# A hybrid decoder step on one core: attention's first tiles, mask and ones placed outside the staging memory

## The reference

```python
def stick_breaking_weights(z, mask):
    log_beta = jax.nn.log_sigmoid(z)
    log_1m = jnp.where(mask, jax.nn.log_sigmoid(-z), 0.0)
    ax = z.ndim - 1
    tail = lax.cumsum(log_1m, axis=ax, reverse=True) - log_1m
    return jnp.where(mask, jnp.exp(log_beta + tail), 0.0)

def block(args):                       # 128 queries, all keys
    q_blk, start = args
    z = einsum('bqhd,bkhd->bhqk', q_blk, k) * scale + bias
    mask = kpos[None, :] < (start + arange(128))[:, None]
    a = stick_breaking_weights(z, mask)
    return einsum('bhqk,bkhd->bqhd', a, v)
```

## Time and profile before

| | |
|---|---|
| median of 3 runs | 2984.35 us (2983.45 to 2986.84) |
| the profiled execution | 2984.83 us, its span 2983.1 us |
| busy, share of the span | PE 93%, PEld 89%, DVE 43%, POOL 35%, ACT 22% |
| granted TensorE clock, mean | 0.95 |
| chain that ended last | PE 82%, DVE 9%, issue 5%, ACT 3% |
| Q projection to first attention matmul | about 1571 to 1654 us |
| attention, 144 chunks | about 1654 to 1937 us |
| decode step | about 1937 to 2091 us |

### The profile page before, as it was taken

The page is one execution under the profiler, slowest core; times in us unless marked ns, Lnnn a source line. Parts: engine busy times, 40 slices in busy tenths (PEclk is TensorE's granted clock), DMA queues, the critical chain, the costliest instruction groups (busy, mean ns, idle before and its releaser), DMA issues.

```text
span 2983.1 us, 42739 instructions
## 1 busy us (share of the span) xinstructions
PE 2786.8 (93%) x16800; PEld 2646.7 (89%) x16800; DVE 1278.5 (43%) x2082; ACT 647.0 (22%) x1248; POOL 1036.2 (35%) x742
## 2 busy tenths in 40 slices
PE   4999859999999999989999899989999999999997
PEld 3777529899999999989989799978989999999997
DVE  6589975522222222264133688700352222222226
ACT  4111134300000000023122688700130000000002
POOL 2267952132322232222222566601223322233220
PEclk9999879999999999999999899955999999999999
DMA  3000001021111111114415434243101111111111
GB/s 125 26 19 28 8 36 43 22 64 43 44 49 43 43 45 55 43 39 143 139 51 153 124 104 114 61 145 106 43 24 62 43 50 43 43 43 52 48 43 59
DMA packets 80413, 184.08 MB, mean 62 GB/s; under 512 B 25811, under 2 KB 40531, under 8 KB 79988
## 3 DMA queue, kind: packets, MB, share of 16 engines
q1 hardware_dynamic: 56980, 145.00, 15.7%
q10 hardware_dynamic: 23264, 36.61, 4.1%
HBM read 150.59 MB, written 30.99 MB: 61 GB/s over the span
## 4 chain that ended last, share of the span: by engine, by line
PE 82%; DVE 9%; issue 5%; ACT 3%; POOL 0%; ACTq 0%; DVEq 0%; DMA 0%; SPq 0%; POOLq 0%
PE bank L1179 50%; PE bank L1283 15%; PE bank L1384 4%; DVE cv L937 3%; PE bank L1368 2%; PE bank L1440 2%; PE bank L1412 2%; PE bank L1224 1%; PE bank L1355 1%; PE bank L1356 1%; DVE xg L882 1%; DVE xl L886 1%; DVE ssq L872 1%; PE bank L1246 0%; DVE x L1153 0%
## 5 line engine op out<-in xcount | busy, mean ns | idle before, releaser
L1179 PE MATMUL bank<-xh,wh 128*128 128x352 f32 x3456 | 1130.6, 327 | 32.5 <-DVE xl L886 22.9
L1179 PE MATMUL bank<-xh,wl 128*128 128x352 f32 x3456 | 1116.2, 323 | 0.0
L1179 PE MATMUL bank<-xl,wh 128*128 128x352 f32 x3456 | 1116.1, 323 | 0.0
L489 POOL CAST wh<-w_raw 128x1024 fp32r<-128x1024 f32 x188 | 282.7, 1503 | 1654.4 <-PE bank L1179 1394.4
L1179 PEld LDWEIGHTS bank<-xh,wh 128*128 128x128 f32 x3456 | 654.3, 189 | 45.4 <-DVE xl L886 18.3
L1179 PEld LDWEIGHTS bank<-xl,wh 128*128 128x128 f32 x3456 | 656.7, 190 | 1.8 <-issue 1.7
L1179 PEld LDWEIGHTS bank<-xh,wl 128*128 128x128 f32 x3456 | 655.4, 190 | 0.0
L491 POOL TENSOR_TENSOR wl<-w_raw,wh 128x1024 fp32r<-128x1024 f32 x188 | 456.3, 2427 | 15.0
L1004 DVE TENSOR_TENSOR bank<-bank,sg 128x352 f32<-128x352 f32 x132 | 70.3, 532 | 793.0 <-ACT sg L708 793.0
L1283 PE MATMUL bank<-hh,wh 128*128 128x352 f32 x1056 | 343.7, 326 | 16.4 <-DVE x L1015 13.8
L1283 PE MATMUL bank<-hl,wh 128*128 128x352 f32 x1056 | 339.5, 321 | 0.0
(11 more groups left out here) (145 smaller groups left out, 2550.6 us busy)
## 6 DMA issues: line engine op xcount, KB each, us to landing
w_raw<-wstream SPq DMA_DIRECT2D x188, 512.0 KB, 3.4
k_sb<-k_split SPq DMA_DIRECT2D x16, 512.0 KB, 3.5
kp<-cache_kt SPq DMA_DIRECT2D x16, 512.0 KB, 3.6
vp<-cache_v SPq DMA_DIRECT2D x16, 512.0 KB, 3.6
x<-x_t ACTq DMA_DIRECT2D x3, 1408.0 KB, 12.1
k_t<-stage ACTq DMA_DIRECT2D x8, 528.0 KB, 2.8
y_t<-x ACTq DMA_DIRECT2D x24, 176.0 KB, 2.0
k_split<-stage_h ACTq DMA_DIRECT2D x16, 256.0 KB, 4.6
```

The lines of the kernel that those rows point to most:

```text
L489: pool.tensor_copy(wh[:, s], w_raw[:, s % RAW]).then_inc(w_hi, 1)
L1179: mm = pe.matmul(out, a[:, slot, w], b[:, k, tgs(tg)], start=(k == 0 and i == 0), stop=(k == KC - 1 and i == 2))
```

## The change

The staging memory is overlaid in another way. Two of the four sigmoid tiles (`s_first`, chunks with g % 4 of 0 and 1), the mask and head 0's k lie outside `stage`, `stage_h` and `stage_l`; the other two sigmoid tiles (`s_late`), `at_sb`, and head 1's k and q lie over them. `mask_r` takes the memory of `neg_one`, which moves to the tiles of the decode step and is written there by POOL. DVE's memsets of the ones and of `zero` move ahead of its part of the Q projection, its wait for the stores is gone, and ACT waits for the stores ahead of the third chunk's sigmoid (g == 2).

```diff
--- before.py
+++ after.py
@@ -184,7 +184,7 @@
     mean_w = sb("mean_w", [P, P])
     ident = sb("ident", [P, P])
     neg_tri = sb("neg_tri", [P, P])
-    neg_one = sb("neg_one", [P, P])
+    mask_r = sb("mask_r", [P, P], F32R)
     ident_r = sb("ident_r", [P, P], F32R)
     rstd = sb("rstd", [P, T])
     ssq = sb("ssq", [P, T])
@@ -207,15 +207,16 @@
         stage_l = sb("stage_l", [P, 2, SEQ], F32R, r)
         vn = sb("vn", [P, 6, QT], F32, r)
     with ExitStack() as r:
-        s_sb = sb("s_sb", [P, NZ, QT], F32, r)
+        s_late = sb("s_late", [P, 2, QT], F32, r)
         at_sb = sb("at_sb", [P, AT_TILES, QT], F32, r)
+        k1_sb = sb("k1_sb", [P, SEQ], F32R, r)
         q1_sb = [sb("q1h_sb", [P, SEQ], F32R, r), sb("q1l_sb", [P, SEQ], F32R, r)]
-        mask_r = sb("mask_r", [P, P], F32R, r)
-
-        sb("gap", [P, 448], F32, r)
-        k_sb = sb("k_sb", [P, 2, SEQ], F32R, r)
+
+        sb("gap", [P, 576], F32, r)
+        k0_sb = sb("k0_sb", [P, SEQ], F32R, r)
         v_sb = sb("v_sb", [P, SEQ // P, 3 * DH], F32, r)
         q0_sb = [sb("q0h_sb", [P, SEQ], F32R, r), sb("q0l_sb", [P, SEQ], F32R, r)]
+        s_first = sb("s_first", [P, 2, QT], F32, r)
         b_sb = sb("b_sb", [P, H], F32, r)
         nb_sb = sb("nb_sb", [P, H], F32, r)
         zero = sb("zero", [P, 1], F32, r)
@@ -226,11 +227,13 @@
         vnew = sb("vnew", [NS, D], F32, r)
         b_dec = sb("b_dec", [1, QT], F32, r)
         one_row = sb("one_row", [1, P], F32, r)
+        neg_one = sb("neg_one", [P, P], F32, r)
         pages = sb("pages", [1, 2 * NB], I32, r)
         ds_sb = sb("ds_sb", [P, 3, QT], F32, r)
     da_sb = ds_sb
 
-    q_sb = [q0_sb, q1_sb]
+    q_sb, k_sb = [q0_sb, q1_sb], [k0_sb, k1_sb]
+    s_sb = [s_first[:, 0], s_first[:, 1], s_late[:, 0], s_late[:, 1]]
 
 
     rest_tiles = [ssq[:], xg[:].rearrange("p a t -> p (a t)"), rstd[:]]
@@ -424,7 +427,7 @@
         def load_head(it, e):
             h, used = 2 * it + e, PAIR * (it - 1) + NCHUNK * (e + 1)
             wait_count(sp, Att.z, used)
-            sp.dma_start(k_sb[:, e].bitcast(F32), k_scr[h].rearrange("s d t -> (s d) t")).then_inc(Att.k_in[e], 16)
+            sp.dma_start(k_sb[e][:].bitcast(F32), k_scr[h].rearrange("s d t -> (s d) t")).then_inc(Att.k_in[e], 16)
             for part in range(2):
                 for half in range(2):
                     sp.dma_start(q_sb[e][part][DH * half:DH * half + DH, :].bitcast(F32), q_scr[h, part])\
@@ -469,7 +472,7 @@
         pool.memset(eps[:, 0:1], RMS_EPS).then_inc(consts, 1)
         pool.memset(eps[:, 1:2], LN_EPS).then_inc(consts, 1)
         pool.memset(mean_w[:], 1.0 / D).then_inc(consts, 1)
-        pool.memset(neg_one[:], -1.0).then_inc(consts, 1)
+        pool.sem_inc(consts, 1)
         pool.memset(ident[:], 0.0).then_inc(const_steps, 1)
         pool.memset(neg_tri[:], -1.0).then_inc(const_steps, 1)
         pool.wait_ge(const_steps, 2)
@@ -546,7 +549,7 @@
             pool.wait_ge(Att.sig, g + 1)
             pool.wait_ge(Att.rest, g + 1)
             for seg in chunk(g):
-                tile = s_sb[:, g % NZ, seg.cols]
+                tile = s_sb[g % NZ][:, seg.cols]
                 ins = pool.tensor_tensor(tile, rest(seg, seg.low * P + 1, seg.n * P), tile, ALU.mult)
             ins.then_inc(Att.a, 1)
 
@@ -556,6 +559,7 @@
 
         pool.wait_ge(Att.o_lo, H)
         pool.memset(one_row[:], 1.0).then_inc(Dec.one, 1)
+        pool.memset(neg_one[:], -1.0).then_inc(Dec.one, 1)
 
         def dec_mask(done, tile):
             v = tile.rearrange("p (c b e q) -> p c b e q", c=KC, b=NB, e=2)
@@ -796,7 +800,10 @@
             it, e, h = place(g)
             act.wait_ge(Att.z, g + 1)
             wait_count(act, Att.turn, g + 1 - NZ)
-            act.activation(s_sb[:, g % NZ], Z[g % NZ][:], ACT.Sigmoid, bias=b_sb[:, h:h + 1]).then_inc(Att.sig, 1)
+            if g == 2:
+                for n in range(2):
+                    act.wait_ge(q_stored[n], 4 * 16 * (KC // 2))
+            act.activation(s_sb[g % NZ], Z[g % NZ][:], ACT.Sigmoid, bias=b_sb[:, h:h + 1]).then_inc(Att.sig, 1)
             act.activation(Z[g % NZ][:], Z[g % NZ][:], ACT.Sigmoid, bias=nb_sb[:, h:h + 1], scale=-1.0)\
                .then_inc(Att.keep, 1)
 
@@ -1069,6 +1076,11 @@
 
 
         v.wait_ge(q_zero, 1)
+        v.memset(zero[:], 0.0)
+        for tile in rest_tiles:
+            v.memset(tile[:, SEQ:SEQ + 1], 1.0)
+        for qb, base in SMALL_REST.items():
+            v.memset(small_rest[:, base + (qb + 1) * P:base + (qb + 1) * P + 1], 1.0)
         for c, tg in PAIR_FIRST:
             stage_lo(l_q, c, tg)
             if tg == NTG - 1:
@@ -1107,15 +1119,8 @@
              .then_inc(Att.o_lo, 1)
 
 
-        for n in range(2):
-            v.wait_ge(q_stored[n], 4 * 16 * (KC // 2))
         v.wait_ge(Att.mask_src, 2)
         v.tensor_copy(mask_r[:], mask_src)
-        v.memset(zero[:], 0.0)
-        for tile in rest_tiles:
-            v.memset(tile[:, SEQ:SEQ + 1], 1.0)
-        for qb, base in SMALL_REST.items():
-            v.memset(small_rest[:, base + (qb + 1) * P:base + (qb + 1) * P + 1], 1.0)
         v.wait_ge(Att.b_in, 16)
         v.tensor_scalar(nb_sb[:], b_sb[:], -1.0, None, ALU.mult).then_inc(Att.const, 2)
         v.wait_ge(Att.const, 2)
@@ -1350,7 +1355,7 @@
                 pe.wait_ge(Att.q_in[e], it * 64 + 64)
             wait_count(pe, Att.rest, g + 1 - NZ)
             for seg in chunk(g):
-                out, keys = Z[g % NZ][:, seg.cols], k_sb[:, e, seg.low * P:(seg.low + seg.n) * P]
+                out, keys = Z[g % NZ][:, seg.cols], k_sb[e][:, seg.low * P:(seg.low + seg.n) * P]
                 queries = slice(seg.qb * P, (seg.qb + 1) * P)
                 pe.matmul(out, q_sb[e][0][:, queries], keys, start=True, stop=False)
                 mm = pe.matmul(out, q_sb[e][1][:, queries], keys, start=False, stop=True)
@@ -1365,7 +1370,7 @@
             wait_count(pe, Att.at[g % 2], g // 2)
             for b in range(QT // P):
                 cols = slice(b * P, (b + 1) * P)
-                mm = pe.transpose(TB[g % 2][:, cols], s_sb[:, g % NZ, cols], ident[:])
+                mm = pe.transpose(TB[g % 2][:, cols], s_sb[g % NZ][:, cols], ident[:])
             mm.then_inc(Att.turn, 1)
 
         def att_av(g):
@@ -1401,7 +1406,7 @@
 
 
         pe.wait_ge(Dec.new_in, 48)
-        pe.wait_ge(Dec.one, 1)
+        pe.wait_ge(Dec.one, 2)
         for i, rows in ((0, P), (1, P), (2, NS)):
             pe.matmul(Z[i][0:rows, :], one_row[0:1, 0:rows], b_dec[:], start=True, stop=True)
         for n in range(2 * NB):
```

## The result

| | before | changed |
|---|---|---|
| median of 14 runs each, us | 2986.14 (2983.45 to 2988.65) | 2979.15 (2976.11 to 2980.41) |
| the profiled execution / its span | 2984.83 / 2983.1 | 2976.11 / 2974.4 |
| mean granted clock | 0.950 | 0.954 |

The ratio is 0.9976, with a 95% interval of 0.9968 to 0.9984: faster by 0.24%, or 7.0 us between the medians. The forecast time was 2979.3. The forecast gain was 5.1, from a before of 2984.35 that 14 runs put at 2986.14.

What follows compares the result with a forecast made beforehand. TensorE, busy 93% of the span, bounds the kernel; of its 11.3 us wait before attention, ACT's queue limits the gain. Terms -5.37 + 0.25 = -5.1 us, from 2984.35 to 2979.3 us; range 2977.5 to 2981.5.

Steps and rivals of the forecast that it cites:

- the first term: Start of attention: ACT's queue is free at 1649.61, so table load and first sigmoid come earlier, -5.37 us.
- The first rival: Start of attention: sigmoids start with the first z tile and the whole 8.8 us comes back, 2975.6; chance 0.04.
- The second term: First transposes of attention: they start at TensorE's low clock after a stall, +0.25 us.
- the part of 0.63 us: Second chunk's transposes: 0.63 us late because the first chunk's PE work runs at the low clock.
- my bounds: Clock term at attention's first transposes: -0.23 to +0.97 us, from high clock 3.4 or 5.8 us after restart.
- The third rival: Attention's first transposes: the clock stays low 5.8 us from the restart or more, gain 4.4, 2980.0; chance 0.15.
- The third chunk's wait: ACT's new wait for the stores ahead of the third sigmoid: cost 0, margin 0.5 us.
- The second rival: ACT's third sigmoid: the last store lands after 6 us, costing 1.1 us, 2980.4; chance 0.10.
- Costs put at nothing: DVE's memsets, `neg_one` before decoding and head 1's k loads: each cost 0; slower from new tile addresses: chance 0.02.
- Within 0.2%: Whole kernel: the change stays within 0.2%, about 6.0 us, of the time before; chance 0.72.

Runs made afterwards that it cites:

- the places alone: Changed kernel with its new tile places and moved memsets, but DVE again waits for the stores ahead of the mask and ACT doesn't: 2985.09 us, ratio 0.9999.
- the repeat: The changed kernel run once more without an edit, against the kernel before: 2979.55 us, ratio 0.9981.

## Why the prediction was right, and where it was not

*The limit and the first term.* "... the wait looks worth 8.8 us ... The queue of ACT says that it is not": right. The shift of the first sigmoid is 5.41 us (13.95 - 8.54) against a forecast of 5.37, and the run in which SP issues the last four stores shows that the issues on ACT were what held it: with that alone it comes 4.1 us earlier still (4.48). With all eight moved and the table early it comes at 3.70, behind the first z tile. One reading was wrong, though no term used it: k does not lie in memory of the stage buffers in the kernel before, where `k_sb` begins behind `stage_l`. The first rival (all 8.8 us) fails by its own condition, since the eight issues take as long with PE at work beside them (7.17 us after the last matmul, 7.18 before the change).

*The second term, TensorE's clock.* The mechanism was right and the size was off. The transposes started at 1.2 GHz, after 7.4 us without work in the first profile, where the z tiles ran at 2.4 GHz, and 5.87 in the second (forecast 5.6), and the second ones came 1.88 us behind the first and not 1.24, so the part of 0.63 us was right (0.64). The mis-sized step is "I choose 4.4 as the value of the same place": the clock rose 2.7 us after the restart in one profile and 3.4 in the other. The term was +0.25; by the rule of the table it is 0.64 + 0.44 - 1.64 = -0.56 in the first profile and 0.64 + 0.77 - 1.64 = -0.23 in the second. That gives gains of 5.9 and 5.6 at head 1, which the traces show (28.66 - 22.73 = 5.93 and 28.66 - 23.02 = 5.64). The first value lies outside my bounds; a restart can get the high clock sooner than the rows that I took from the kernel before showed (3.4 to 5.8 us). The third rival, a clock that stays low for 5.8 us or more, did not come.

*The third chunk's wait.* Forecast: no cost, 0.5 us of margin. The stores had landed by 10.38, when SP issued head 1's load, and the sigmoid was due at 10.84: 0.46. But "each microsecond beyond the margin would cost a whole one" is wrong. A wait of 2.51 us cost about 0.3, and one of 0.82 nothing. With the longer wait, PE's first stop behind it is not for the third chunk. It is for the first one's copy into `at_sb`, which stands behind the third and fourth sigmoids on ACT (run with the last four stores by SP):

```profile
1654.64 0.61 ACT L822 ACTIVATE at_sb<-bank 128x512 f32<-128x512 f32 x1
...
1655.40 1.13 PE L1397 MATMUL bank<-at_sb,v_sb 128*128 128x128 f32 x8 [0.18 <-ACT at_sb L822]
```

In the changed kernel the same two rows have room:

```profile
1654.34 0.60 ACT L814 ACTIVATE at_sb<-bank 128x512 f32<-128x512 f32 x1 [0.47 <-PE bank L1373]
...
1656.46 1.10 PE L1389 MATMUL bank<-at_sb,v_sb 128*128 128x128 f32 x8
```

ACT waits 0.47 us for the transposes ahead of the copy, and the copy is done 1.5 us before PE reads it (1656.46 - 1654.94). Of the 0.3 us that the longer wait cost, PE's row shows 0.18 as idle time; the rest I can't place. I estimate from these rows that the third sigmoid has about 2 us to spare there, while the first has none. The second rival was priced at 1.1 us; by this estimate it would have cost close to nothing.

*Costs put at nothing* (memsets, `neg_one`, head 1's loads, new addresses): right, by the rows above and by the run with the places alone.

*The total.* The two comparisons give 7.0 and 5.7 us; the traces show 5.6 to 5.9 us at this place. By the totals alone the forecast gain of 5.1 is not refuted, since the interval of the first ratio runs from 4.8 to 9.6 us; it is the traces that show it too small, by 0.5 to 0.8 us. The spans of the first pair differ by 8.7, of which 1.8 arose before the last projection matmul (1642.43 against 1640.62) and 1.0 behind head 1's first matmul (2983.1 - 1671.09 = 1312.0 against 2974.4 - 1663.35 = 1311.0). In the repeat of the changed kernel both are gone: 1643.50 at the projection's end, and 2978.4 - 1666.52 = 1311.9 behind. Over all ten profiles the projection ends between 1640.62 and 1644.24, and 1311.0 to 1313.0 us lie behind head 1's first matmul, in no order that follows the edits. I take both for scatter between executions; what makes it wasn't tried, and whether something of the 7.0 is real beyond 5.9 stays open.

That 2979.3 came so close to 2979.15 is in part luck: the before that it started from (2984.35, three runs) was 1.8 us too low, and the gain, by the first comparison, 1.9 us too small. The repeat is the fairer measure: 2979.55, with a gain of 5.7. "Within 0.2%" was a close call, as the text said. The time stayed above its border of 2978.4, but the first ratio is a gain of 0.24% with an interval from 0.16 to 0.32, which crosses the border; in the repeat it is 0.19%.

## What to carry to other kernels

Before a wait is priced, look at what else stands in the queue of the engine that acts next: here PE's idle time of 11.3 us was worth only 5.4, because ACT spent 7.1 us in issuing DMAs. Such issues belong to an engine that has nothing to do: with SP issuing the last four, head 1 came 3.4 us earlier than in the changed kernel's first profile, and with all eight on SP, the table early and the wait later, 5.7. Here the first chunk was on the path while the third had slack, so a wait that must stand somewhere is worth trying as late as the memory allows. What a late wait costs is read from the work that stands behind it in the same engine's program, here the copy of an earlier chunk. A pause of TensorE should be charged for the slow stretch behind it.

## What the runs showed of the hardware

- A DMA issue of 64 partitions x 4 KB holds ACT's queue for 0.45 to 1.2 us, and the eight last together for 7.1 us, the same in all profiles in which ACT issues them. Some issues of the same size take twice as long as others; why was not tried.
- A table load that was placed between such issues ran beside them: 1.28 us from 1643.50, with the issues on both sides of it in time, and the last one ended at 7.10 as without it (7.12 to 7.18).
- I read the stores' landing from the start of SP's next load, which waits for it. It came 3.2 us after the end of the last store's issue in the changed kernel (10.38 - 7.17) and with all eight on SP (7.63 - 4.38), and 3.6 and 3.4 us after it in the two runs with the last four on SP. Here an issue that ended sooner let the stores land sooner by about as much.
- The clock's rise came 2.7 and 3.4 us after the same restart in two profiles of one program, and its first fall once before and once after the z tiles. One profile is no measure of such a term.
- An ACT table load took 1.28 us in each profile, and where its input was there the sigmoid behind it started 0.01 to 0.02 us later. The Trainium skill ("ScalarE: Activation LUTs", section "What ACT_TABLE_LOAD costs") gives 2.66 us for a switch with its drain. The measured 1.28 decides here; in the two runs that load the table early, the load also began within 0.02 us of the end of ACT's last copy.
